# Joining the two exponential maps of a differential head before they are turned, and scaling queries instead of scores

## What is computed

```
s  = einsum('bqhmd,bkhmd->bmhqk', q, k) * scale        # m: two maps
p  = softmax(s, axis=-1)
pd = p[:, 0] - lam * p[:, 1]                           # one number lam for all
o  = einsum('bhqk,bkhd->bqhd', pd, v)
out = rmsnorm(o, subln_g) * (1 - lam_init)
```

## Time and profile before

| | us |
|---|---|
| median of 3 runs | 4312.69 (4307.73 to 4315.8) |
| profiled execution, its own time | 4315.09 |
| its span | 4313.2 |
| TensorE matmul busy | 4206.6 (98%) |
| VectorE busy | 3057.1 (71%) |
| ScalarE busy | 1799.7 (42%) |
| mean granted clock of TensorE | 0.992 |
| differential steps of the even mixer | about 1847 to 1908 |
| its neighbourhood steps | about 1908 to 1956 |

### The profile page before, as it was taken

The page is one execution under the profiler, slowest core; times in us unless marked ns, Lnnn a source line. Parts: engine busy times, 40 slices in busy tenths (PEclk is TensorE's granted clock), DMA queues, the critical chain, the costliest instruction groups (busy, mean ns, idle before and its releaser), DMA issues.

```text
span 4313.2 us, 61906 instructions
## 1 busy us (share of the span) xinstructions
PE 4206.6 (98%) x24423; PEld 3743.7 (87%) x24423; DVE 3057.1 (71%) x5064; ACT 1799.7 (42%) x2992; POOL 1333.8 (31%) x699
## 2 busy tenths in 40 slices
PE   7999999999999999999999999999999999999999
PEld 5888778888888799867999999899999799998887
DVE  5775558877887686465589777788887675554776
ACT  3233352233233535164243777333334645444444
POOL 0000300000000100000378666767772048544443
PEclk9999999999999999999999999999999999999999
DMA  7543214544645364202477899999994156778884
GB/s 276 221 161 150 79 53 193 221 185 189 234 181 202 117 245 171 98 21 69 136 244 247 287 331 339 369 365 359 352 355 178 60 196 216 226 246 280 288 288 167
DMA packets 287202, 926.39 MB, mean 215 GB/s; under 512 B 19648, under 2 KB 171328, under 8 KB 212800
## 3 DMA queue, kind: packets, MB, share of 16 engines
q1 hardware_dynamic: 250048, 788.18, 51.3%
q0 software_dynamic: 36864, 134.23, 8.8%
HBM read 837.40 MB, written 84.93 MB: 214 GB/s over the span
## 4 chain that ended last, share of the span: by engine, by line
PE 83%; DMA 6%; DVE 5%; ACT 3%; POOL 1%; issue 1%; SPq 0%; ACTq 0%; POOLq 0%; DVEq 0%
PE bank L1132 24%; PE bank L1134 24%; PE bank L1133 24%; DMA gates<-work 4%; PE bank L1563 2%; PE bank L1325 2%; PE bank L1127 1%; PE bank L1332 1%; PE bank L1122 1%; PE bank L1118 1%; POOL weight_ring_low L2887 1%; PE bank L1357 1%; DVE work L2616 1%; DVE weight_ring_low L2232 1%; DMA work<-in_up_rows,work 1%
## 5 line engine op out<-in xcount | busy, mean ns | idle before, releaser
L2887 POOL TENSOR_TENSOR weight_ring_low<-weight_ring,up_high 128x1024 fp32r<-128x1024 f32 x233 | 589.3, 2534 | 1102.3 <-ACT up_high L1980 1099.7
L1134 PE MATMUL bank<-peer_h_high,weight_ring_low 128*128 128x256 f32 (+2 forms) x2240 | 698.0, 312 | 0.0
L1132 PE MATMUL bank<-peer_h_high,up_high 128*128 128x384 f32 (+1 forms) x2048 | 642.8, 314 | 14.7 <-POOL weight_ring_low L2887 8.7
L1133 PE MATMUL bank<-h_low,up_high 128*128 128x384 f32 (+1 forms) x2048 | 633.5, 309 | 0.0
L2067 ACT ACTIVATE down_high<-weight_ring 128x1024 fp32r<-128x1024 f32 x256 | 257.1, 1052 | 522.6 <-PE bank L1134 516.4
L1134 PE MATMUL bank<-h_high,weight_ring_low 128*128 128x512 f32 (+1 forms) x1280 | 464.0, 362 | 0.0
L1132 PE MATMUL bank<-h_high,in_high 128*128 128x512 f32 (+1 forms) x1216 | 441.1, 363 | 0.3
L1133 PE MATMUL bank<-h_low,in_high 128*128 128x512 f32 (+1 forms) x1216 | 440.8, 362 | 0.0
L2851 POOL TENSOR_SCALAR h<-work,params 128x256 f32<-128x256 f32 x12 | 11.8, 998 | 1377.1 <-PE bank L1470 874.7
L1134 PEld LDWEIGHTS bank<-peer_h_high,weight_ring_low 128*128 128x128 f32 x2240 | 426.1, 190 | 3.7
L2643 DVE TENSOR_TENSOR weight_ring_low<-weight_ring,down_high 128x1024 fp32r<-128x1024 f32 x128 | 309.8, 2420 | 157.2 <-ACT down_high L2067 157.2
(11 more groups left out here) (417 smaller groups left out, 10118.4 us busy)
## 6 DMA issues: line engine op xcount, KB each, us to landing
weight_ring<-in_up SPq DMA_DIRECT2D x128, 1024.0 KB
weight_ring<-in_down SPq DMA_DIRECT2D x128, 1024.0 KB
weight_ring<-in_mod_w SPq DMA_DIRECT2D x112, 1024.0 KB
weight_ring<-in_ffn_in SPq DMA_DIRECT2D x88, 1024.0 KB
weight_ring<-in_ffn_out SPq DMA_DIRECT2D x64, 704.0 KB
gates<-work SPq DMA_DIRECT2D x40, 1024.0 KB, 10.0
gelu<-work SPq DMA_DIRECT2D x64, 384.0 KB
work<-gates SPq DMA_DIRECT2D x32, 768.0 KB, 13.2
```

The source lines that it names most:

```text
L1132: mm(dst, w_high, a_high, start=first, stop=False)
L1133: mm(dst, w_high, a_low, start=False, stop=False)
L1134: return mm(dst, w_low, a_high, start=False, stop=last)
L2887: G.tensor_tensor(ring_low[:, slot, w], ring[:, slot, w], up_high[:, n % 3, :].bitcast(F32), ALU.subtract)\
```

## The change

For a differential pair, VectorE joins the two maps of exponentials before they are turned: with sums s1 and s2 of the two rows it makes factor = -lambda * s1 / s2 and writes e1 + factor * e2 over e1. TensorE turns and multiplies this one tile. VectorE then scales the output by 1 / s1. So a pair has one turn, one copy of a turned tile, one output, one normalise. The turn of a pair now stands at its odd step, behind the output of the pair before and the scores of steps i + 3 and i + 4; ScalarE's copy at the odd step, behind the exponential of step i + 2; the normalise at the even step i for pair (i - 3) // 2. The exponential that reuses the buffer of a second map waits for the join, one that reuses that of a first map for the turn. The third exponential of the even mixer waits for the last value panel, whose weights lie in its buffer. VectorE has one operation less in each maximum except in the odd mixer: the reduce negates its result. For this, scores must carry their scale already: the scale goes into the queries of the differential and the latent heads as they are copied or rotated out of their banks. The core of the diff:

```
+        probs_joined = sem("probs_joined")
...
                 def turn(i):
                     m, j, r = m0 + i, jobs[step_at(i)[0]], turns_before(name, i)
-                    pe.wait_ge(exp_done, m + 1)
+                    if i < 4 * ns:
+                        pe.wait_ge(probs_joined, i // 2 + 1)
+                        src = probs[:, (m - 1) % 4]
+                    else:
+                        pe.wait_ge(exp_done, m + 1)
+                        src = probs[:, m % 4]
...
                 for i in range(n + 4):
-                    if i < n:
+                    if 4 * ns <= i < n:
                         turn(i)
                     if i % 2:
                         for k in range(i + 3, min(i + 5, n)):
                             scores(k)
-                    if 2 <= i < 4 * ns + 2:
+                    if i % 2 and 3 <= i < 4 * ns + 2:
                         sub_outs(i - 2)
+                    if i % 2 and i < 4 * ns:
+                        turn(i)
                     elif i % 2 and 4 * ns + 3 <= i < n + 2:
                         outs(i - 2)
...
                     act.wait_ge(max_ready, m + 1)
-                    if i >= 4:
+                    if i >= 4 and i - 4 < 4 * ns and i % 2:
+                        act.wait_ge(probs_joined, (i - 4) // 2 + 1)
+                    elif i >= 4:
                         act.wait_ge(probs_turned, turns_before(name, i - 4) + 1)
+                    if ns and i == 2:
+                        act.wait_ge(panel_done, proj_panel(name))
...
-                    if i < n:
+                    if 4 * ns <= i < n:
                         copy_turned(i)
...
                     if i + 2 < n:
                         exp(i + 2)
+                    if i % 2 and i < 4 * ns:
+                        copy_turned(i)
...
-                        V.tensor_scalar(neg_max[:, k:k + 1], row_max[:, k:k + 1], -scale, None, ALU.mult).then_inc(max_ready, 1)
+                        V.tensor_reduce(neg_max[:, k:k + 1], bank[:, 0:j["nk"]], AX, ALU.max, negate=True).then_inc(max_ready, 1)
+
+                def join_probs(i):
+                    m, nk = m0 + i, jobs[step_at(i)[0]]["nk"]
+                    k, first, second = m % 8, probs[:, (m - 1) % 4, 0:nk], probs[:, m % 4, 0:nk]
+                    factor = row_inv[:, k:k + 1]
+                    dve.wait_ge(exp_done, m + 1)
+                    link(V.reciprocal(row_inv[:, k - 1:k + 1], row_sum[:, k - 1:k + 1]))
+                    link(V.scalar_tensor_tensor(factor, factor, neg_lam, row_sum[:, k - 1:k], ALU.mult, ALU.mult))
+                    V.scalar_tensor_tensor(first, second, factor, first, ALU.mult, ALU.add).then_inc(probs_joined, 1)
 
                 def normalise_sub(i):
-                    link(V.reciprocal(row_inv[:, k:k + 1], row_sum[:, k:k + 1]))
-                    inv = row_inv[:, k:k + 1]
-                    dst = sub_rows[:, p, t, :]
-                    if i % 2:
-                        link(V.tensor_tensor(inv, inv, neg_lam, ALU.mult))
-                        dve.wait_ge(rows_ready, i)
-                        V.scalar_tensor_tensor(dst, src, inv, dst, ALU.mult, ALU.add).then_inc(rows_ready, 1)
-                    else:
-                        V.tensor_scalar(dst, src, inv, None, ALU.mult).then_inc(rows_ready, 1)
+                    V.tensor_scalar(sub_rows[:, i // 4, t, :], ps[6 + i // 2 % 2][:, 0:P], row_inv[:, k - 1:k], None, ALU.mult)\
+                        .then_inc(rows_ready, 1)
...
+                    if i % 2 and i < 4 * ns:
+                        join_probs(i)
                     if i + 3 < n:
                         maximum(i + 3)
-                    if 3 <= i < 4 * ns + 3:
+                    if i % 2 == 0 and 4 <= i < 4 * ns + 3:
                         normalise_sub(i - 3)
...
-                    i = V.tensor_copy(mla_q[0:NOPE, hd, 0:t], ps[p % BANKS][half, 0:t])
+                    i = V.tensor_scalar(mla_q[0:NOPE, hd, 0:t], ps[p % BANKS][half, 0:t], QK ** -0.5, None, ALU.mult)
...
-                p = rotated_chunks(name, s, p, df_q, 4, True)
+                p = rotated_chunks(name, s, p, df_q, 4, True, HD ** -0.5)
```

More of the change, by code:

```diff
@@ L547, in build @@
         counts = dict(norm=0, added=0, ffn=0, free=4, square=0, root=0, lora=0, conv=0, tile=0, out=0, mod=0,
-                      peer=0, ptile=0, rtile=0, parts=0, scaled=0, normed=0, rounds=0, keys=0, context=0, pv=0, summed=0, joined=0, sub=0)
+                      peer=0, ptile=0, rtile=0, parts=0, scaled=0, normed=0, rounds=0, keys=0, context=0, pv=0, summed=0, joined=0, turn=0)
         take = scratch()
@@ L805, in squares_of, with job @@
             return ps[4 + k % 2][:, :] if s["before"] == "ffn" else work[:, (1 + k % 2) * T:(2 + k % 2) * T]
-        def job(q, k, nk, v, scale, prep=None):
-            return dict(q=q, k=k, nk=nk, v=v, scale=scale, prep=prep)
+        def job(q, k, nk, v, prep=None):
+            return dict(q=q, k=k, nk=nk, v=v, prep=prep)
         def q_tiles(ap, n0):
@@ L829, in even_jobs @@
                                         head_half(df_k, m, hd, keys), 128 * len(kbs),
-                                        [df_v[:, kb, P * hd:P * hd + P] for kb in kbs], HD ** -0.5))
+                                        [df_v[:, kb, P * hd:P * hd + P] for kb in kbs]))
                     subs.append(h[:, 4 + hd, n0:n0 + TL])
@@ L835, in even_jobs @@
                                     head_half(na_k, hd % 2, hd // 2, keys), 128 * len(kbs),
-                                    [na_v[:, kb, HD * hd:HD * hd + HD] for kb in kbs], 1.0, ("na", hd) if n0 == 0 else None))
+                                    [na_v[:, kb, HD * hd:HD * hd + HD] for kb in kbs], ("na", hd) if n0 == 0 else None))
                 dsts += [h[:, c, n0:n0 + TL] for c in range(NA_H // 2)]
@@ L845, in odd_jobs @@
                                 head_half(sw_k, n % 2, n // 2, slice(0, T)), T,
-                                [sw_v[:, kb, HD * n:HD * n + HD] for kb in range(4)], 1.0, ("swa", hd)))
+                                [sw_v[:, kb, HD * n:HD * n + HD] for kb in range(4)], ("swa", hd)))
             return jobs, [h[:, c, LAT] for c in range(KC)], []
@@ L874, in turns_before @@
             ns = len(job_lists[name][2])
-            return at[name]["tile"] + at[name]["sub"] + i + sum(back_slot(ns + q) < i for q in range(ns))
+            steps_turned = i // 2 if i < 4 * ns else i - 2 * ns
+            return at[name]["turn"] + steps_turned + sum(back_slot(ns + q) < i for q in range(ns))
         def turns_before_sub(name, q):
             jobs, dsts, subs = job_lists[name]
-            return at[name]["tile"] + at[name]["sub"] + min(2 * len(jobs), back_slot(len(subs) + q) + 1) + q
+            return at[name]["turn"] + min(2 * len(jobs), back_slot(len(subs) + q) + 1) - 2 * len(subs) + q
         def conv_rounded_at(name, j):
@@ L950, in build @@
                 counts["out"] += len(job_lists[name][1])
-                counts["sub"] += len(job_lists[name][2])
-                counts["pv"] += 2 * len(job_lists[name][0]) - 2 * len(job_lists[name][1])
+                counts["turn"] += 2 * len(job_lists[name][0]) - len(job_lists[name][2])
+                counts["pv"] += len(job_lists[name][0])
         block = ctx.enter_context(nc.Block())
@@ L1337, in sub_outs @@
                     pe.wait_ge(turned_copied, turns_before(name, i) + 1)
-                    wait_for(pe, rows_ready, i - 1)
+                    wait_for(pe, rows_ready, i // 2 - 1)
                     nb, dv = j["nk"] // P, j["v"][0].shape[1]
                     for kb in range(nb):
-                        o = mm(ps[6 + m % 2][:, 0:dv], turned[:, m % 4, kb, :], j["v"][kb], start=kb == 0, stop=kb == nb - 1)
+                        o = mm(ps[6 + i // 2 % 2][:, 0:dv], turned[:, m % 4, kb, :], j["v"][kb], start=kb == 0, stop=kb == nb - 1)
                     o.then_inc(outs_done, 1)
@@ L1945, in mix_stage @@
                         for j in range(4):
-                            i = A(mla_q[NOPE:QK, 4 * c + j, CTX], ps[(18 + c) % BANKS][ROPE * j:ROPE * j + ROPE, CTX], ACT.Copy)
+                            i = A(mla_q[NOPE:QK, 4 * c + j, CTX], ps[(18 + c) % BANKS][ROPE * j:ROPE * j + ROPE, CTX], ACT.Copy, scale=QK ** -0.5)
                         i.then_inc(context_copied, 1)
@@ L2377, in maximum @@
                     j = jobs[job]
-                    k, bank, scale = m % 8, ps[m % 4], j["scale"]
+                    k, bank = m % 8, ps[m % 4]
                     dve.wait_ge(scores_done, m + 1)
@@ L2546, in rotated_chunks @@
                     if ctx_too:
-                        steps.count(V.tensor_copy(dst[:, c, CTX], ps[p % BANKS][:, CTX]))
+                        steps.count(V.tensor_scalar(dst[:, c, CTX], ps[p % BANKS][:, CTX], scale, None, ALU.mult))
                     a, b = rope(name, p, slice(0, P), HD // 4, param("cos2"), param("sin2"), scale)
```

21 lines of the change are left out of this document (9 added, 12 removed).

## The result

The changed kernel takes 4291.44 us (median of 5 runs, 4287.59 to 4295.98), the kernel before 4312.69 (5 runs, 4305.43 to 4320.28). The ratio is 0.9950 with a 95% interval of 0.9937 to 0.9964: 21 us faster, and clear of noise. The prediction was 4293, range 4286 to 4303.

A forecast was written before the change was run, and what follows sets the result against it. Pairs over 512 keys were taken as TensorE bound, those over 256 as bound by a chain with two VectorE links. Gains summed to 20.0 us: 4315.1 - 20.0 = 4295.1, 4293 on the median's scale; range 4286 to 4303.

The forecast's parts named there:

- start: From the last value panel's copy into the differential pairs: next scores at 1851.65 instead of 1855.10, gain 3.4 us.
- four long periods: Differential pairs over 512 keys, 1855.10 to 1871.66: 16.56 us becomes 10.6, gain 6.0.
- mixed: Differential pairs between those over 512 and 256 keys, 1871.66 to 1881.16: 9.50 us becomes 6.3, gain 3.2.
- five short: Differential pairs over 256 keys, 1881.16 to 1895.07: 13.91 us becomes 9.0, gain 4.9.
- two on the way into the neighbourhood heads: Pairs from 1895.07 to 1903.17, 8.10 us: set by VectorE at 3.2 each, gain 1.7.
- the last: From 1903.17 to the first paired output at 1908.11, 4.94 us: gain 0.8.
- Long pairs: Differential pairs over 512 keys: TensorE bound, 4.14 us becomes 2.60, 2.65 with signals; VectorE at 2.50.
- Short pairs: Differential pairs over 256 keys: 2.79 us becomes 1.80 with signals; VectorE 1.74 passes TensorE 1.40.
- Long pairs before: Differential pairs over 512 keys in the kernel before: every piece of the 4.14 us is TensorE.
- Rival A: Differential pairs: VectorE bound, operations not overlapping, 3.0 us over 512 keys, 2.25 over 256; gain 14, median 4299; chance 0.22.
- Rival B: Differential pairs: in-order queue makes loops one pair long, 4.3 and 3.1 us; no change, median 4315; chance 0.07.
- C: TensorE's clock falls to 1.2 GHz in 256-key pairs, stays low until the stage's output; 9 us slower, 4322; chance 0.04.

The follow-up runs named there:

- turn twice: The changed kernel with every turn of a differential pair done twice into the same bank; 4294.1 us.
- half the join: The changed kernel with the join over only the first half of the columns; 4294.3 us.
- both experiments on VectorE: Two variants of the changed kernel: joining done in two operations instead of one, 4299.8 us; joining only the first half of the columns, 4294.3 us.
- Scaling only: The kernel before with the scale in the queries and the negating maximum, no join; 4313.1 us beside 4311.2.
- join only: The changed kernel without the scaling of the queries: scale back in the exponential, second small operation back in every maximum; 4298.0 us.
- turn first: The changed kernel with each differential pair's turn moved ahead of the scores and output before it in TensorE's queue; 4330.2 us, kernel before 4311.2.

## Why the prediction was right, step by step

- **Sum.** Predicted gain 20.0 us in the mixer, measured 20.6. By the prediction's terms, with the scores' weight loads in the trace after at 1851.25, 1861.59, 1868.40, 1876.98 and 1883.25: start 3.3 (3.4 predicted), four long periods 6.2 (6.0), mixed 2.7 (3.2), five short 5.3 (4.9), two on the way into the neighbourhood heads 1.8 (1.7), the last 1.2 (0.8). The total is closer than its terms: the mixed pairs gave 0.5 less, and the short ones and the last together 0.8 more, so part of the agreement is luck.
- **Long pairs**, 2.65 predicted, 2.59 measured; "turn twice" and "half the join" show that this is TensorE's own work. The 0.05 that I added for signals wasn't needed. That VectorE would almost tie was right: 2.57 against the predicted 2.50, since the join costs 0.75 (0.70 taken, 0.75 the upper end of its bounds) and the one-column factor 0.25 from start to start (0.20 taken).
- **Short pairs**, 1.80 predicted, 1.77 measured, and VectorE's, as predicted and as both experiments on VectorE show. TensorE's own part, put at 1.40, is 1.49. The first of the five periods was only 1.51, TensorE's own need; that is over half of the 0.4 above the term.
- **Long pairs before: a wrong reading that didn't hurt.** "Every piece is TensorE" took the chain at its word. "Scaling only" shows that at least 0.19 of the 4.14 was the wait for VectorE's normalise. The subtraction 4.14 - 1.53 came out right since the removed output and its wait went together. As a statement on what the scaling alone does it was wrong: 3.0 us from A, not the "up to 0.5, taken as nothing" outside the join. With the join beside it, the scaling is worth 5.5 of the 20.6, as "join only" shows, since it takes 0.19, and not the 0.1 that I counted before that run, off each maximum on the engine that has become the bound. Together the two parts are worth more than their sum: the join alone 15.1, the scaling alone 3.0, both 20.6. In the latent mixers, which lie ahead of A, the scaling shows nothing: the last value panel is copied at 1846.1 before and 1845.6 after, and at 1845.6 to 1847.5 over the nine executions.
- **Mixed pairs** were 0.5 us longer than predicted. I had set them at TensorE's sum, 2.17. In the chain after, the turned tile's copy on ScalarE stands in it: with scores of 0.63 in place of 1.06 between turn and output, the copy is no longer covered.

```profile
1863.57 0.44 PE bank L1337 x4
1864.00 0.72 PE bank L1325 x4
...
1864.75 1.16 PE bank L1346 x8
1865.91 0.45 PE bank L1337 x4
...
1866.44 0.60 ACT work L1882
...
1867.09 1.17 PE bank L1346 x8
```

- **Rival A**, VectorE in full and nothing overlapping: two maxima of 0.69 take 1.28 together in the timeline after, so independent operations do overlap. Where the next one needs the result, they don't, and a signal of 0.02 to 0.04 comes on top. The Trainium skill (VectorE: DVE Perf Modes, "The DRAIN you can't avoid") lets the next operation start only once the pipe is empty, but adds that one that isn't held starts earlier. The independent operations here agree with the second (0.60 from start to start for a reduce of 0.68). The dependent ones can't tell the two apart, since the program makes each of them wait for a semaphore of its predecessor. The rival took the first for all of them.
- **Rival B and C** didn't occur, and "turn first" shows that both were near: B is avoided by the turn's place in the queue, and not by the four buffers on which the prediction relied, so on this point it was right for a reason that doesn't hold. The periods there, 4.47 and 3.02, were close to the 4.3 and 3.1 that I gave. The clock stayed at 1.00 through all pairs in the trace of the changed kernel, and fell only where it fell before (0.67 from 1932 to 1936 in the trace after). In four of the experiments it fell behind the table loads as well, at a cost of about 1.5 us.
- **What follows is only moved.** From the first paired output to the output projection it is 48.0 us before and after, in these two traces. The table loads are as long as before, 1.28 us each.

## What to carry to other kernels

When work is taken off the bounding engine and part of it is put on another, add up that other engine's queue from start to start, letting an operation that needs its predecessor's result start only at that one's end and a signal later; the sums for VectorE here were then within 0.07 us of the measured pairs, and the one that missed this rule ("join only") came to 3.1 us where 5.5 were measured. Buffers don't decouple engines if one in-order queue holds the waiting instruction ahead of work that others wait for: walk each loop through the queues in their order, also through instructions that only stand in between. Test the reading "bound by this engine" with twice and half of one operation, since a trace can write a wait down as work.

## What the runs showed of the hardware that I had not expected

- A scalar_tensor_tensor out of SBUF takes 0.75 us for 512 columns and 0.48 for 256, so about 1.05 ns a column and 0.22 fixed; on one column it takes 0.22, where tensor_tensor takes 0.16 and the reciprocal 0.15.
- A dependent small operation behind a 512-wide maximum costs 0.19 us (0.79 for 0.60): the reduce loses its overlap of 0.08 with its successor, a signal takes 0.03, and the operation itself, of 0.15, another 0.08.
- TensorE's granted clock went to 0.50 at 1890.4 of the "turn first" kernel, although from 1857 on TensorE never stood still for longer than 1.7 us at a time (nine waits of a turn for the join, 1.3 to 1.7 each), and stayed there for the remaining short pairs.
- The same instructions behind the same waits met the full clock in one execution (the changed kernel at 1894.8) and the lower one in another ("half the join" at 1894.5), at a price of 1.6 us for a turn, the scores and an output.
